# Expert rows stored and gathered, against rows added to the output by indirect accumulating transfers

## The chip, the cores and the metric

The kernel runs on one core of a Trainium2 chip. The metric is the device time of one execution in microseconds; the kernel before was timed three times: 2560.4 us median, 2554.97 to 2566.02.

## The reference, cut to what matters

The program is two transformer blocks over 256 tokens of 2048 features in fp32. The last stage of the second block is a mixture of experts. Each token goes to one group of 8 experts out of 4 groups and, inside it, to the two experts with the largest logits; each expert is a gated layer 2048 -> 256 -> 2048.

```
weights = softmax(top_val) * p_group                  # (token, 2)
act     = silu(xb @ w_gate[e]) * (xb @ w_up[e])       # rows of expert e
ys      = act @ w_down[e]
m       = sum over the token's 2 rows of weights * ys
x       = x + gate2 * m                               # the output
```

Everything ahead of this stage is untouched by the change.

## The kernel before, in words

The stage is cut into 48 tiles of 32 rows. Each of the 32 experts has one tile (even numbers of experts at tile % 3 == 0, odd ones at tile % 3 == 2), and the 16 tiles with tile % 3 == 1 are spare ones for rows beyond 32 of an expert. Which expert a spare serves is known only on the chip; where it serves none, its weights are not loaded, yet the tile is computed all the same on what lies in the buffer, and its rows are used by nobody.

A tile needs three weight units of 2 MB: two for gate and up, one for down. They live in `moe_raw`, two slots of three units: slot 0 serves tiles 3i and 3i+1, slot 1 serves tiles 3i+2. SyncE's queue loads the experts' tiles (L2797), each unit as soon as its slot is free (L2840: `e.free`), and GpSimd issues the spares' loads under a condition (L2801), after tile 3i has used the same units (L2849).

TensorE's order per tile: `up` on two units (L2876, 32-row weights, four row strips of PSUM, one for each quarter of the contraction), `fold` that adds the four strips (L2887), `down` (L2899), and between them `gather`, which picks the rows of a later tile out of the normalized tokens by a one-hot product (L2866, L2867). `down` puts output columns 512q to 512q+511 of its 32 rows into strip q of one bank, 128 partitions by 512. ScalarE makes `part` (L2958) and `silu` (L2952). VectorE makes `hidden` (L3021), half of the `spread` (L3014), the one-hot `places` (L2991, L2995), and `take` (L3027), which multiplies the tile's output by the gate and puts it into one of eight `moe_stage` buffers.

The stage buffer is stored to a DRAM tensor `expert_rows` of 1536 rows by four transfers per tile that ScalarE issues (L2964), two tiles later in its order. After the last tile a second block follows: GpSimd waits for all stores, and gathers for each half of the tokens and each of the two choices 128 rows of 8 KB by an indirect transfer (L3059); VectorE multiplies them by the token's weight and adds them to `x` (L3069); SyncE writes `x` to the output (L3080) and waits for it.

Of the kernel before, what the change touches and what calls it, by code (L numbers as in the profile page):

```python
# [43 lines left out]
MOE_SLOTS = MOE_TILES * ROWS  # L44
MOE_SPARE = MOE_TILES - EXPERTS
D_EXPERT = 256
MOD_COLS = 6 * D
# [22 lines left out]
for _name, _n in (("slot", MOE_SLOTS), ("fold", ROWS), ("steps", 7), ("start", EXPERTS),  # L70
                  ("jump", EXPERTS), ("earlier", EXPERTS + 1), ("tile", 1)):
    MOE[_name] = (_at, _n)
    _at += _n
# [76 lines left out]
def bank(k, b):  # L150
    return k.psum[:, b, :]
# [2399 lines left out]
class Sorting:  # L2551
# [6 lines left out]
    def __init__(self, sb):  # L2558
        self.const = sb("sorting", [P, N_MOE])
        self.slot = sb("slot_of", [P, TT, 2])  # L2560
        self.weight = sb("weight_of", [P, TT, 2])
        self.row = sb("row_of", [P, TT, 2], dtype=mybir.dt.int32)
        self.spare_of, self.filled = (sb(n, [P, 1], dtype=mybir.dt.int32) for n in ("spare_of", "spare_filled"))
# [6 lines left out]
def route(nc, k, x, x_t, xn_hi, router, scope_sb, first_loads):  # L2570
# [88 lines left out]
    with nc.Block(no_gpsimd_drain=True) as block:  # L2659
        @block.vector  # L2660
        def _(dve):
# [62 lines left out]
            s.settle()  # L2724
            s.step(dve.tensor_copy(sorting.row[:], sorting.slot[:]))

# [32 lines left out]
class Experts:  # L2759
# [9 lines left out]
    def __init__(self, k, weights, sb, sem):  # L2769
        self.k, self.weights = k, weights  # L2770
        self.raw = sb("moe_raw", [P, 2, self.UNITS, UNIT])
        self.unit_in = [[sem(f"moe_unit_in{slot}_{u}") for u in range(self.UNITS)] for slot in range(2)]
        self.spare_in = [sem(f"moe_spare_in{u}") for u in range(self.UNITS)]
        self.used_up, self.used_down, self.parts = sem("moe_used_up"), sem("moe_used_down"), sem("moe_parts")
        self.folded, self.silu_done, self.hid_done = sem("moe_folded"), sem("moe_silu_done"), sem("moe_hid_done")
        self.gathered, self.x_act, self.x_dve = sem("moe_gathered"), sem("moe_x_act"), sem("moe_x_dve")
        self.staged, self.y_done, self.x_low = sem("moe_staged"), sem("moe_y_done"), sem("moe_x_low")
        self.row_in = [sem(f"moe_row_in{n}") for n in range(2 * TT)]
        self.stored = [sem(f"moe_stored{n}") for n in range(self.STAGED)]

    def buffers(self, sb):
        self.place = sb("moe_place", [P, 2, TT, P], dtype=F32R)
        self.x_t = sb("moe_x_t", [P, 2, KC, P])
        self.part, self.silu = sb("moe_part", [P, 2, COLS]), sb("moe_silu", [P, 2, 2, ROWS])
        self.hid, self.stage = sb("moe_hid", [P, 2, 2, ROWS]), sb("moe_stage", [P, self.STAGED, COLS])

    @staticmethod
# [27 lines left out]

def experts(nc, k, io, e, x, xn_hi, xn_lo, sorting, scale, shift, gate_rows):
    s = k.dve_steps
    quads = MOE_TILES // 4
# [13 lines left out]
    def strip(n):  # L2832
        return slice(ROWS * n, ROWS * n + ROWS)
    with nc.Block(no_gpsimd_drain=True) as block:
        @block.sync
        def _(sp):
            for n in range(3, MOE_TILES):
                if n % 3 != 1:
                    for u in range(e.UNITS):
                        e.free(sp, n - 2 if n % 3 == 0 else n - 3, u)  # L2840
                        e.load(sp, n, u)

        @block.gpsimd
        def _(pool):
            for i in range(MOE_SPARE):
                at = pool.value_load(sorting.spare_of[i:i + 1, 0:1], min_val=0, max_val=e.UNITS * (EXPERTS - 1))
                filled = pool.value_load(sorting.filled[i:i + 1, 0:1], min_val=0, max_val=1)
                for u in range(e.UNITS):
                    e.free(pool, 3 * i, u)  # L2849
                    e.load_spare(pool, 3 * i + 1, u, at, filled)  # L2850

        @block.tensor
        def _(pe):
# [26 lines left out]
            def fold(tile):  # L2880
                pe.wait_ge(e.parts, tile + 1)
                if tile >= 2:
                    pe.wait_ge(e.hid_done, tile - 1)
# [7 lines left out]
            def down(tile):  # L2891
# [5 lines left out]
                for c in range(2):  # L2897
                    for q in range(4):
                        mm = pe.matmul(outs(tile)[strip(q), :], e.hid[:, tile % 2, c, :],  # L2899
                                       w[:, c * D + q * COLS:c * D + (q + 1) * COLS], start=c == 0, stop=c == 1)  # L2900
                mm.then_inc(e.used_down, 1)
            for g in range(3):
                gather(g)
            for tile in range(MOE_TILES):
# [14 lines left out]
                if shared_next:  # L2919
# [17 lines left out]
        def _(act):  # L2937
# [21 lines left out]

            def store(tile):  # L2960
                act.wait_ge(e.y_done, tile + 1)
                at = ROWS * Sorting.ORDER[tile]
                for q in range(4):
                    act.dma_start(io["rows"][at:at + ROWS, q * COLS:(q + 1) * COLS], e.stage[strip(q), tile % e.STAGED])\  # L2964
                       .then_inc(e.stored[tile % e.STAGED], 16)
            for g in (0, 2):
                spread(g)
            for tile in range(MOE_TILES):
# [5 lines left out]
                if tile % 2 == 0 and tile + 4 < MOE_TILES:  # L2974
                    spread(tile + 4)
                if tile >= 2:
                    store(tile - 2)
            silu(MOE_TILES - 1)
            store(MOE_TILES - 2)
            store(MOE_TILES - 1)  # L2980

        @block.vector
        def _(dve):
# [48 lines left out]
            places(1)  # L3032
            spread(3)
            for tile in range(MOE_TILES):
                if tile and tile % 3 != 1:
                    hidden(tile - 1)
                if tile % 3 == 0:
                    if tile:
                        take(tile - 1)
                    hidden(tile)  # L3040
                if tile % 2 and tile + 4 < MOE_TILES:
                    spread(tile + 4)
# [7 lines left out]
            take(MOE_TILES - 1)  # L3050
    rows = [[e.raw[:, 0, c, t * D:(t + 1) * D] for c in range(2)] for t in range(TT)]
    with nc.Block(no_gpsimd_drain=True) as block:
        @block.gpsimd
        def _(pool):
            for n in range(e.STAGED):
                pool.wait_ge(e.stored[n], 64 * len(range(n, MOE_TILES, e.STAGED)))
            for t in range(TT):
                for c in range(2):
# [4 lines left out]
        @block.vector  # L3063
        def _(dve):
            s.eng = dve
            for t in range(TT):
                for c in range(2):
                    dve.wait_ge(e.row_in[2 * t + c], 16)
                    ins = dve.scalar_tensor_tensor(x[:, t, :], rows[t][c], sorting.weight[:, t, c:c + 1], x[:, t, :],  # L3069
                                                   ALU.mult, ALU.add)  # L3070
                    if c == 0:
                        s.step(ins)
                        s.settle()
                ins.then_inc(k.out_ready, 1)

        @block.sync
        def _(sp):
            for t in range(TT):
                sp.wait_ge(k.out_ready, t + 1)
                sp.dma_start(io["out"][t * P:(t + 1) * P, :], x[:, t, :]).then_inc(k.out_written, 16)  # L3080
            sp.wait_ge(k.out_written, 16 * TT)


def program(nc, io):
    k = Kit(io["stream"])
    with ExitStack() as ctx:
# [7 lines left out]
        def sem(name):  # L3094
# [10 lines left out]
            sem("act_sem"), sem("pe_sem"), sem("consts_in")  # L3105
        k.out_ready, k.out_written, k.small_in = \
            sem("out_ready"), sem("out_written"), sem("small_in")
        k.row_high, k.row_low, k.row_used = sem("row_high"), sem("row_low"), sem("row_used")
# [189 lines left out]
        xn_hi, xn_lo = (sb(n, [P, TT, D], dtype=F32R) for n in ("xn_hi", "xn_lo"))  # L3298
        sorting = router.sorting
# [4 lines left out]
        experts(nc, k, io, moe, x, xn_hi, xn_lo, sorting, lambda c: scale2[:, c:c + 1],  # L3304
                lambda c: mod_cols[:, 32 + c:33 + c], gate_rows)
# [3 lines left out]
def lay_out(a):  # L3309
# [45 lines left out]
    for level in range(6):  # L3355
# [24 lines left out]
        "jump": np.broadcast_to(ROWS * (EXPERTS - 1 - experts), (P, EXPERTS)),  # L3380
        "earlier": m < np.arange(EXPERTS + 1), "tile": m,
    }
# [33 lines left out]
```

## Time and profile before

| What | Value |
|---|---|
| Median of three timed runs | 2560.4 us |
| Profiled execution, own time | 2563.39 us |
| Its span, first to last instruction | 2561.7 us |
| Mean granted TensorE clock | 0.918 of full speed |
| TensorE matmuls / VectorE / ScalarE / GpSimd busy | 2274.2 / 1331.5 / 789.4 / 21.5 us |
| Expert stage with its routing | from 1967 us to the end |

The span is what the profile's rows cover; some 1.7 us of the execution's own time lie outside it. Busy times are of the whole kernel and say little of one stage, so the rows below are mostly of stretches: the expert stage's steady part, one of its periods of three tiles, its start and its end. DMA share is the mean busy share of the 16 DMA engines.

### The profile page before, as it was taken

How to read it: one execution, taken by the hardware profiler on the slowest of the kernel's cores; microseconds unless marked ns; L12 is line 12 of the kernel's file. 1: busy time of each engine (PE TensorE's matmuls, PEld its weight loads, DVE VectorE, ACT ScalarE, POOL GpSimd, SP SyncE). 2: the span in 40 equal slices, each digit the busy share in tenths (PEclk: the TensorE clock that was granted, in tenths of full speed). 3: DMA queues.
4: the chain of work that ended last, by engine and by line, in shares of the span. 5: the costliest groups of instructions: out<-in, count | busy, mean ns of one | idle time of the engine just before them, and what ended most of it. 6: DMA issues, size and time to landing. Idle time of an engine off the chain costs nothing. (4 is left out here: it accounts for less than half of the span.)

```text
span 2561.7 us, 39746 instructions
## 1 busy us (share of the span) xinstructions
PE 2274.2 (89%) x17030; PEld 1832.3 (72%) x17030; DVE 1331.5 (52%) x1580; ACT 789.4 (31%) x917; POOL 21.5 (1%) x62
## 2 busy tenths in 40 slices
PE   7998799878889988999999999997978768888885
PEld 7998799677867657899999998976854424444441
DVE  4776655564453126878787978855543301111112
ACT  4444333311143024434334334345431101111110
POOL 0000000000000000000000000000000000000000
PEclk8999899887889998999999999998989768899987
DMA  4453034100053317888897888824522899999998
GB/s 201 184 197 132 2 131 197 58 2 1 2 207 154 132 66 273 325 320 322 303 356 300 338 327 325 343 107 196 197 84 106 330 418 420 427 423 428 426 427 337
DMA packets 68150, 610.05 MB, mean 238 GB/s; under 512 B 9614, under 2 KB 9870, under 8 KB 16782
## 3 DMA queue, kind: packets, MB, share of 16 engines
q1 hardware_dynamic: 56906, 572.11, 55.9%
q0 software_dynamic: 1872, 23.07, 2.2%
q10 hardware_dynamic: 9216, 12.60, 1.4%
q8 instruction: 121, 1.98, 0.3%
q14 instruction: 35, 0.29, 0.0%
HBM read 674.85 MB, written 14.68 MB: 269 GB/s over the span
## 5 line engine op out<-in xcount | busy, mean ns | idle before, releaser
L2051 ACT ACTIVATE ffn_w_hi<-ffn_raw 128x2048 fp32r<-128x2048 f32 x128 | 245.0, 1916 | 372.1 <-PE psum L2096 368.8
L2058 DVE TENSOR_TENSOR ffn_w_lo<-ffn_raw,ffn_w_hi 128x2048 fp32r<-128x2048 f32 x128 | 292.3, 2287 | 90.9 <-ACT ffn_w_hi L2051 90.9
L2094 PE MATMUL psum<-u_hi,ffn_w_hi 128*128 128x256 f32 x1024 | 294.0, 287 | 15.0 <-DVE ffn_w_lo L2058 13.9
L2876 PE MATMUL psum<-moe_raw,moe_x_t 128*32 128x512 f32 x1536 | 219.3, 703 | 83.9 <-DMA moe_raw<-in_moe 76.4
L2096 PE MATMUL psum<-u_hi,ffn_w_lo 128*128 128x256 f32 x1024 | 293.3, 286 | 0.0
L2095 PE MATMUL psum<-u_lo,ffn_w_hi 128*128 128x256 f32 x1024 | 293.3, 286 | 0.0
L613 DVE SCALAR_TENSOR_TENSOR shared<-mod_raw,c_silu,shared 128x2048 f32<-128x2048 f32 x96 | 225.0, 2344 | 0.0
L2094 PEld LDWEIGHTS psum<-u_hi,ffn_w_hi 128*128 128x128 f32 x1024 | 200.4, 196 | 15.8 <-DVE ffn_w_lo L2058 14.1
L2095 PEld LDWEIGHTS psum<-u_lo,ffn_w_hi 128*128 128x128 f32 x1024 | 200.3, 196 | 0.4
L2096 PEld LDWEIGHTS psum<-u_hi,ffn_w_lo 128*128 128x128 f32 x1024 | 200.2, 195 | 0.0
L2094 PE MATMUL psum<-ffn_w_hi,ffn_hid_hi 128*128 128x512 f32 x512 | 199.5, 390 | 0.0
L2095 PE MATMUL psum<-ffn_w_lo,ffn_hid_hi 128*128 128x512 f32 x512 | 199.4, 389 | 0.0
L2096 PE MATMUL psum<-ffn_w_hi,ffn_hid_lo 128*128 128x512 f32 x512 | 199.2, 389 | 0.0
L2876 PEld LDWEIGHTS psum<-moe_raw,moe_x_t 128*32 128x32 f32 x1536 | 49.1, 120 | 194.5 <-issue 154.1
L320 PE MATMUL psum<-dn_u_hi,dn_w_hi 128*128 128x256 f32 x512 | 146.5, 286 | 0.0
L322 PE MATMUL psum<-dn_u_hi,dn_w_lo 128*128 128x256 f32 x512 | 145.8, 285 | 0.0
L321 PE MATMUL psum<-dn_u_lo,dn_w_hi 128*128 128x256 f32 x512 | 145.8, 285 | 0.0
L3021 DVE TENSOR_TENSOR moe_hid<-moe_silu,psum 128x64 f32<-128x64 f32 x48 | 10.6, 221 | 213.0 <-ACT moe_silu L2952 213.0
L320 PE MATMUL psum<-rw_u_hi,rw_w_hi 128*128 128x256 f32 x384 | 110.1, 287 | 9.7 <-DVE rw_w_lo L309 9.7
L2866 PEld LDWEIGHTS psum<-moe_place,xn_hi 128*128 128x128 f32 x384 | 79.0, 206 | 46.7 <-issue 44.1
L2094 PEld LDWEIGHTS psum<-ffn_w_hi,ffn_hid_hi 128*128 128x128 f32 x512 | 96.2, 188 | 20.1
L2096 PEld LDWEIGHTS psum<-ffn_w_hi,ffn_hid_lo 128*128 128x128 f32 x512 | 96.1, 188 | 20.1
(579 smaller groups left out, 4344.5 us busy)
## 6 DMA issues: line engine op xcount, KB each, us to landing
moe_raw<-in_moe SPq DMA_DIRECT2D x96, 2048.0 KB, 17.2
ffn_raw<-in_ffn SPq DMA_DIRECT2D x128, 1024.0 KB, 5.5
ring<-in_stream SPq DMA_DIRECT2D x59, 2048.0 KB, 12.1
mod_raw<-in_mod SPq DMA_DIRECT2D x96, 1024.0 KB, 7.4
moe_raw<-in_moe POOLq DMA_DIRECT2D x48, 2048.0 KB
expert_rows<-moe_stage ACTq DMA_DIRECT2D x192, 64.0 KB, 8.5
x<-in_x SPq DMA_DIRECT2D x2, 1024.0 KB, 5.9
u<-in_mem SPq DMA_DIRECT2D x2, 1024.0 KB, 15.3
```

What stands on the lines that cost most here:

```text
L320: pe.matmul(out, hi, self.u_hi[:, chunk, :], start=chunk == 0, stop=False)
L321: pe.matmul(out, hi, self.u_lo[:, chunk, :], start=False, stop=False)
L322: mm = pe.matmul(out, lo, self.u_hi[:, chunk, :], start=False, stop=chunk == KC - 1)
L613: dve.scalar_tensor_tensor(at, self.raw[:, i % self.RAWS], self.c_silu[:, c:c + 1], at, ALU.mult, ALU.add)\
L2051: act.activation(self.w_hi[:, number % self.HIGHS], self.raw[:, number % self.RAWS], ACT.Copy)\
L2058: dve.tensor_tensor(self.w_lo[:, number % self.LOWS], self.raw[:, number % self.RAWS], self.w_hi[:, number % self.HIGHS].bitcast(F32), ALU ...
L2094: pe.matmul(out, lhs[0], rhs[0], start=start, stop=False)
L2095: pe.matmul(out, lhs[0], rhs[1], start=False, stop=False)
L2096: return pe.matmul(out, lhs[1], rhs[0], start=False, stop=stop)
L2866: pe.matmul(gathers(piece)[:, c, :], xn_hi[:, t, own], rows, start=t == 0, stop=False)
L2876: mm = pe.matmul(summed(tile)[strip(q), :], e.x_t[:, tile // 4 % 2, UNIT_KC * u + c, strip(tile % 4)], w[:, c * COLS:(c + 1) * COLS], star ...
L3021: dve.tensor_tensor(e.hid[:, tile % 2], e.silu[:, tile % 2], folds(tile)[:, 1], ALU.mult).then_inc(e.hid_done, 1)
```

## The change

Instead of 48 stored row blocks and a gather at the end, the unweighted residual `x` is written to the output at the start of the stage, and each tile adds its own rows to the output in memory.

- `Sorting` keeps each token's rank within its expert (`rank`) and no longer the integer row (`row`); the constants get a column `quarter`, m // 32 + 2048.
- VectorE runs a new function `hots` once, between `spread(3)` and tile 0: two `token` columns, a few steps on 128x4 values, and for each half of the tokens and each choice three comparisons against constants: a one-hot of the row in its tile (128x128) and two one-hots of the tile (128x48), scaled by the weight and by the token's number.
- TensorE runs `row_tables` once, after the last gather of tile 0's turn and before `down(0)`: four matmuls of 128x128 by 96 columns into a free part of bank 3. VectorE reads them after `hidden(0)`: a weight and an output row for each partition and tile. A row that holds no token gets number 2048 + q or more, which is past the last of the 1024 row quarters of the output.
- `take` becomes one SCALAR_TENSOR_TENSOR that multiplies by the row's weight and by the gate.
- GpSimd issues for every tile one indirect transfer of 128 pieces of 2 KB from the stage buffer to the output, with an add (`compute_op`), which leaves pieces out whose number is past the bound. Each waits until the one before it has landed. They stand in GpSimd's order behind the spare loads of their period: tiles 3i-1, 3i and 3i+1 behind the loads of tile 3i+1, and tile 47 last.
- ScalarE's stores, the DRAM tensor `expert_rows`, and the whole last block are gone; SyncE waits for the last accumulating transfer.

```diff
+    out_rows = io["out"].rearrange("t (q n) -> (t q) n", n=COLS)
+    def scatter(pool, tile):
+        pool.wait_ge(e.y_done, tile + 1)
+        if tile:
+            pool.wait_ge(e.scattered, 16 * tile)
+        pool.indirect_dma_start(out_rows, bass.IndirectOffsetOnAxis(ap=e.row_at[:, tile:tile + 1], axis=0),
+                                e.stage[:, tile % e.STAGED], None, bounds_check=4 * T - 1, oob_is_err=False,
+                                compute_op=ALU.add).then_inc(e.scattered, 16)
         def _(sp):
+            for t in range(TT):
+                sp.dma_start(io["out"][t * P:(t + 1) * P, :], x[:, t, :]).then_inc(k.out_written, 16)
...
+            sp.wait_ge(e.scattered, 16 * MOE_TILES)
         def _(pool):
...
                     e.load_spare(pool, 3 * i + 1, u, at, filled)
+                if i == 0:
+                    pool.wait_ge(k.out_written, 16 * TT)
+                    pool.wait_ge(e.rows_known, 1)
+                for tile in range(max(3 * i - 1, 0), 3 * i + 2):
+                    scatter(pool, tile)
+            scatter(pool, MOE_TILES - 1)
             def fold(tile):
                 pe.wait_ge(e.parts, tile + 1)
+                if tile == 1:
+                    pe.wait_ge(e.rows_known, 1)
+            def row_tables():
+                pe.wait_ge(e.hot_done, 1)
+                for n in range(2 * TT):
+                    mm = pe.matmul(bank(k, 3)[:, 256:256 + 2 * MOE_TILES], hot_row[:, n // 2, n % 2, :],
+                                   hot_tile[:, n // 2, n % 2].rearrange("p v n -> p (v n)"), start=n == 0, stop=n == 2 * TT - 1)
+                mm.then_inc(e.hot_mm, 1)
...
                         gather(tile + 4, range(2, 4))
+                    if tile == 0:
+                        row_tables()
                     down(tile)
-            def store(tile):
-                act.wait_ge(e.y_done, tile + 1)
-                at = ROWS * Sorting.ORDER[tile]
-                for q in range(4):
-                    act.dma_start(io["rows"][at:at + ROWS, q * COLS:(q + 1) * COLS], e.stage[strip(q), tile % e.STAGED])\
-                       .then_inc(e.stored[tile % e.STAGED], 16)
             def take(tile):
                 dve.wait_ge(e.used_down, tile + 1)
                 if tile >= e.STAGED:
-                    dve.wait_ge(e.stored[tile % e.STAGED], 64 * (tile // e.STAGED))
-                dve.tensor_tensor(e.stage[:, tile % e.STAGED], outs(tile), gate_rows[:], ALU.mult).then_inc(e.y_done, 1)
+                    dve.wait_ge(e.scattered, 16 * (tile - e.STAGED + 1))
+                dve.scalar_tensor_tensor(e.stage[:, tile % e.STAGED], outs(tile), e.row_weight[:, tile:tile + 1], gate_rows[:],
+                                         ALU.mult, ALU.mult).then_inc(e.y_done, 1)
+            def hots():
...
+                for t in range(TT):
+                    for c in range(2):
+                        dve.tensor_scalar(hot_row[:, t, c, :].rearrange("p (q r) -> p q r", r=ROWS),
+                                          starts[:, 0:1, :].broadcast_to([P, 4, ROWS]), row[:, t, c:c + 1], None, ALU.is_equal)
+                        dve.tensor_scalar(hot_tile[:, t, c, 0, :], starts[:, :, 0], first_row[:, t, c:c + 1],
+                                          sorting.weight[:, t, c:c + 1], ALU.is_equal, ALU.mult)
+                        ins = dve.tensor_scalar(hot_tile[:, t, c, 1, :], starts[:, :, 0], first_row[:, t, c:c + 1],
+                                                token[:, t:t + 1], ALU.is_equal, ALU.mult)
+                ins.then_inc(e.hot_done, 1)
-    rows = [[e.raw[:, 0, c, t * D:(t + 1) * D] for c in range(2)] for t in range(TT)]
...
-                    pool.indirect_dma_start(rows[t][c], None, io["rows"],
-                                            bass.IndirectOffsetOnAxis(ap=sorting.row[:, t, c:c + 1], axis=0))\
-                        .then_inc(e.row_in[2 * t + c], 16)
...
-                    ins = dve.scalar_tensor_tensor(x[:, t, :], rows[t][c], sorting.weight[:, t, c:c + 1], x[:, t, :],
-                                                   ALU.mult, ALU.add)
...
-                sp.dma_start(io["out"][t * P:(t + 1) * P, :], x[:, t, :]).then_inc(k.out_written, 16)
```

## Rows read from the trace of the kernel before

**Rows 1.** Windows: stretch, its us, busy of each engine, PEclk, DMA share, GB/s
```profile
2000.00:2010.00 10.00, 8.49 (x53) 6.04 (x56) 3.74 (x12) 1.50 (x4) 0.71 (x1) 0.73 0.16 36
2010.00:2042.00 32.00, 27.04 (x224) 12.73 (x220) 4.41 (x13) 7.20 (x16) 1.61 (x3) 0.95 0.93 368
2145.00:2530.00 385.00, 332.67 (x2607) 157.19 (x2602) 63.32 (x169) 55.94 (x142) 1.58 (x36) 0.91 1.01 426
2387.00:2418.00 31.00, 28.11 (x216) 13.72 (x216) 5.25 (x13) 3.74 (x9) 0.13 (x3) 0.90 1.01 428
```
**Rows 2.** Chain of waits, two successive periods: start us, us, what
```profile
2369.69 17.68 DMA moe_raw<-in_moe
...
2400.93 17.98 DMA moe_raw<-in_moe
```
**Rows 3.** The page's DMA queues: packets, MB, share of 16 engines' span
```profile
q0 software_dynamic: 1872, 23.07, 2.2%
q10 hardware_dynamic: 9216, 12.60, 1.4%
```
**Rows 4.** The page's DMA issues: transfer, issuer, count, KB each, us to landing
```profile
moe_raw<-in_moe SPq DMA_DIRECT2D x96, 2048.0 KB, 17.2
...
expert_rows<-moe_stage ACTq DMA_DIRECT2D x192, 64.0 KB, 8.5
```
**Rows 5.** The stores' line L2964 alone, from 2145 us: min/median/max to landing
```profile
DMA to landing us min/median/max: 1.6/8.6/13.9
```
**Rows 6.** Timeline of one period, GpSimd's skipped spare loads and VectorE's takes
```profile
2384.52 0.04 POOL L2801 DMA_DIRECT2D moe_raw<-in_moe  x1 [17.87 <-PE psum L2876]
2391.20 0.04 POOL L2801 DMA_DIRECT2D moe_raw<-in_moe  x1 [6.64 <-PE psum L2876]
2392.83 0.69 DVE L3027 TENSOR_TENSOR moe_stage<-psum,gate_rows 128x512 f32<-128x512 f32 x1 [7.19 <-PE psum L2899]
2397.26 3.62 PE L2876 MATMUL psum<-moe_raw,moe_x_t 128*32 128x512 f32 x32
2397.85 0.04 POOL L2801 DMA_DIRECT2D moe_raw<-in_moe  x1 [6.60 <-PE psum L2899]
...
2411.38 0.69 DVE L3027 TENSOR_TENSOR moe_stage<-psum,gate_rows 128x512 f32<-128x512 f32 x1 [0.52 <-PE psum L2899]
```
**Rows 7.** Timeline of the end
```profile
2519.06 0.69 DVE L3027 TENSOR_TENSOR moe_stage<-psum,gate_rows 128x512 f32<-128x512 f32 x1 [7.14 <-PE psum L2899]
...
2522.91 0.04 POOL L2801 DMA_DIRECT2D moe_raw<-in_moe  x1 [5.48 <-PE psum L2899]
...
2536.91 0.69 DVE L3027 TENSOR_TENSOR moe_stage<-psum,gate_rows 128x512 f32<-128x512 f32 x1 [2.47 <-PE psum L2899]
2541.52 1.00 POOL L3059 DMA_INDIRECT moe_raw<-expert_rows,row_of  x1 [18.57 <-DMA expert_rows<-moe_stage]
...
2547.22 2.35 DVE L3069 SCALAR_TENSOR_TENSOR x<-moe_raw,weight_of,x 128x2048 f32<-128x2048 f32 x1 [9.61 <-DMA moe_raw<-expert_rows,row_of]
...
2552.44 5.30 SPq L3080 DMA_DIRECT2D out<-x  x2
```
**Rows 8.** Timeline of the start: what stands around `hots` and `row_tables`
```profile
1988.91 0.16 DVE L2721 SCALAR_TENSOR_TENSOR slot_of<-of_row 128x4 f32<-128x4 f32 x1
...
2001.49 0.47 DVE L2991 TENSOR_SCALAR moe_place<-sorting,slot_of 128x128 fp32r<-128x128 f32 x2
...
2008.33 1.36 DVE L3014 TENSOR_SCALAR moe_x_t<-psum,scale,mod_cols 128x128 f32<-128x128 f32 x4 [5.72 <-PE psum L2867]
...
2013.95 0.22 DVE L3021 TENSOR_TENSOR moe_hid<-moe_silu,psum 128x64 f32<-128x64 f32 x1 [4.25 <-ACT moe_silu L2952]
```
**Rows 9.** Line L2740: small matmuls, min/median/max ns
```profile
L2740 PE MATMUL psum<-consts,any_of x4: 420/421/421, 1983.8 to 1984.4; 128*32 128x128 f32 x4
```

More of the change, by code:

```diff
@@ L45 @@
 MOE_SPARE = MOE_TILES - EXPERTS
+NO_ROW = 8 * T
 D_EXPERT = 256
@@ L70 @@
 for _name, _n in (("slot", MOE_SLOTS), ("fold", ROWS), ("steps", 7), ("start", EXPERTS),
-                  ("jump", EXPERTS), ("earlier", EXPERTS + 1), ("tile", 1)):
+                  ("jump", EXPERTS), ("earlier", EXPERTS + 1), ("tile", 1), ("quarter", 1)):
     MOE[_name] = (_at, _n)
@@ L2561, in __init__ @@
         self.weight = sb("weight_of", [P, TT, 2])
-        self.row = sb("row_of", [P, TT, 2], dtype=mybir.dt.int32)
+        self.rank = sb("rank_of", [P, TT, 2])
         self.spare_of, self.filled = (sb(n, [P, 1], dtype=mybir.dt.int32) for n in ("spare_of", "spare_filled"))
@@ L2724, in _ @@
             s.settle()
-            s.step(dve.tensor_copy(sorting.row[:], sorting.slot[:]))
+            s.step(dve.tensor_copy(sorting.rank[:], of_row[:, :, :, 0]))
             dve.wait_ge(k.act_sem, k.act_n + 3)
@@ L2777, in __init__ @@
         self.staged, self.y_done, self.x_low = sem("moe_staged"), sem("moe_y_done"), sem("moe_x_low")
-        self.row_in = [sem(f"moe_row_in{n}") for n in range(2 * TT)]
-        self.stored = [sem(f"moe_stored{n}") for n in range(self.STAGED)]
+        self.hot_done, self.hot_mm, self.rows_known = sem("moe_hot_done"), sem("moe_hot_mm"), sem("moe_rows_known")
+        self.scattered = sem("moe_scattered")
     def buffers(self, sb):
@@ L2785, in buffers @@
         self.hid, self.stage = sb("moe_hid", [P, 2, 2, ROWS]), sb("moe_stage", [P, self.STAGED, COLS])
+        self.row_weight, self.row_at = sb("moe_row_weight", [P, MOE_TILES]), sb("moe_row_at", [P, MOE_TILES], dtype=mybir.dt.int32)
     @staticmethod
@@ L2813, in first_loads, with experts @@
                 self.load(sp, n, u)
-def experts(nc, k, io, e, x, xn_hi, xn_lo, sorting, scale, shift, gate_rows):
-    s = k.dve_steps
+def experts(nc, k, io, e, x, xn_hi, xn_lo, router, scale, shift, gate_rows):
+    s, sorting = k.dve_steps, router.sorting
+    spare = router.w_norm[:].rearrange("p c n -> p (c n)")
+    hot_row = spare[:, 0:512].rearrange("p (t c n) -> p t c n", t=TT, c=2)
+    hot_tile = spare[:, 512:512 + 8 * MOE_TILES].rearrange("p (t c v n) -> p t c v n", t=TT, c=2, v=2)
+    over = spare[:, 900:928].rearrange("p (t c n) -> p t c n", t=TT, c=2)
+    earlier, row, first_row = (spare[:, 928 + 4 * n:932 + 4 * n].rearrange("p (t c) -> p t c", t=TT) for n in range(3))
+    token = spare[:, 940:942]
+    out_rows = io["out"].rearrange("t (q n) -> (t q) n", n=COLS)
     quads = MOE_TILES // 4
@@ L2975, in _ @@
                     spread(tile + 4)
-                if tile >= 2:
-                    store(tile - 2)
             silu(MOE_TILES - 1)
-            store(MOE_TILES - 2)
-            store(MOE_TILES - 1)
         @block.vector
@@ new lines, in hots @@
+            def hots():
+                steps, ranks = sorting.of("steps"), sorting.rank[:]
+                starts = sorting.of("slot").rearrange("p (n r) -> p n r", r=ROWS)
+                for t in range(TT):
+                    s.step(dve.tensor_scalar(token[:, t:t + 1], sorting.of("tile"), 4.0, float(4 * P * t - NO_ROW), ALU.mult, ALU.add))
+                s.step(dve.tensor_tensor(over, ranks.unsqueeze(3).broadcast_to([P, TT, 2, 7]),
+                                         steps.unsqueeze(1).unsqueeze(1).broadcast_to([P, TT, 2, 7]), ALU.is_gt))
+                s.settle()
+                s.step(dve.tensor_reduce(earlier, over, AX.X, ALU.add))
+                s.settle()
+                s.step(dve.scalar_tensor_tensor(row, earlier, -float(ROWS), ranks, ALU.mult, ALU.add))
+                s.settle()
+                s.step(dve.tensor_scalar(row, row, -1.0, None, ALU.add))
+                s.settle()
+                s.step(dve.tensor_tensor(first_row, sorting.slot[:], row, ALU.subtract))
+                s.settle()
+                for t in range(TT):
+                    for c in range(2):
[6 more added lines that the diff above has]
+                ins.then_inc(e.hot_done, 1)
@@ L3028, in _, with row_tables @@
+            def row_tables():
+                dve.wait_ge(e.hot_mm, 1)
+                s.step(dve.tensor_copy(e.row_weight[:], bank(k, 3)[:, 256:256 + MOE_TILES]))
+                dve.tensor_scalar(e.row_at[:], bank(k, 3)[:, 256 + MOE_TILES:256 + 2 * MOE_TILES], sorting.of("quarter"), None,
+                                  ALU.add).then_inc(e.rows_known, 1)
+                s.settle()
             places(0)
@@ L3033, in _ @@
             spread(3)
+            hots()
             for tile in range(MOE_TILES):
@@ L3040, in _ @@
                     hidden(tile)
+                    if tile == 0:
+                        row_tables()
                 if tile % 2 and tile + 4 < MOE_TILES:
@@ L3050, in _ @@
             take(MOE_TILES - 1)
-    rows = [[e.raw[:, 0, c, t * D:(t + 1) * D] for c in range(2)] for t in range(TT)]
[L3052 to L3058, printed above, removed]
-                    pool.indirect_dma_start(rows[t][c], None, io["rows"],
-                                            bass.IndirectOffsetOnAxis(ap=sorting.row[:, t, c:c + 1], axis=0))\
-                        .then_inc(e.row_in[2 * t + c], 16)
[L3063 to L3068, printed above, removed]
-                    ins = dve.scalar_tensor_tensor(x[:, t, :], rows[t][c], sorting.weight[:, t, c:c + 1], x[:, t, :],
-                                                   ALU.mult, ALU.add)
[L3071 to L3079, printed above, removed]
-                sp.dma_start(io["out"][t * P:(t + 1) * P, :], x[:, t, :]).then_inc(k.out_written, 16)
-            sp.wait_ge(k.out_written, 16 * TT)
 def program(nc, io):
@@ L3105, in program @@
             sem("act_sem"), sem("pe_sem"), sem("consts_in")
-        k.out_ready, k.out_written, k.small_in = \
-            sem("out_ready"), sem("out_written"), sem("small_in")
+        k.out_written, k.small_in = sem("out_written"), sem("small_in")
         k.row_high, k.row_low, k.row_used = sem("row_high"), sem("row_low"), sem("row_used")
@@ L3298, in program @@
         xn_hi, xn_lo = (sb(n, [P, TT, D], dtype=F32R) for n in ("xn_hi", "xn_lo"))
-        sorting = router.sorting
         with ExitStack() as routing:
@@ L3303, in program @@
         moe.buffers(sb)
-        experts(nc, k, io, moe, x, xn_hi, xn_lo, sorting, lambda c: scale2[:, c:c + 1],
+        experts(nc, k, io, moe, x, xn_hi, xn_lo, router, lambda c: scale2[:, c:c + 1],
                 lambda c: mod_cols[:, 32 + c:33 + c], gate_rows)
@@ L3380, in lay_out @@
         "jump": np.broadcast_to(ROWS * (EXPERTS - 1 - experts), (P, EXPERTS)),
-        "earlier": m < np.arange(EXPERTS + 1), "tile": m,
+        "earlier": m < np.arange(EXPERTS + 1), "tile": m, "quarter": m // ROWS + NO_ROW,
     }
@@ L3411 @@
     io["out"] = nc.dram_tensor("out", (T, D), F32, kind="ExternalOutput").ap()
-    io["rows"] = nc.dram_tensor("expert_rows", (MOE_SLOTS, D), F32).ap()
     program(nc, io)
```

## The prediction

> **What bounds the kernel now.** I read the stretches first, since the page's busy shares mix stages. In the steady part of the expert stage the DMA share is 1.01 at 426 GB/s, while TensorE is busy 333 of 385 us and VectorE 63 [rows 1]: the 16 DMA engines are full, and time goes by what they carry. The chain of waits says the same: it stands in a load of `moe_raw` for 17.68 us of a period, and the same place comes 31.24 us later [rows 2]. A period is three tiles, two with weights: 6 units of 2.097 MB are 12.58 MB, and 3 tiles of stores 0.79 MB; 13.37 MB in 31.24 us are 428 GB/s, the rate of the row. So the stores displace weights byte for byte, and they are worth reading as time. TensorE's 28.1 busy of 31 us [rows 1] is the next bound, 2.9 us below.
>
> How many spares are filled can be read too: GpSimd's queue moved 23.07 MB [rows 3], of which the last gathers are 4 x 1.05 = 4.19 MB, and 18.87 MB are left, three tiles of 6.29 MB. So 35 of 48 tiles hold rows, 13 periods have an empty spare, 3 a filled one.
>
> The end of the kernel is a serial tail. The last `take` ends at 2537.60; then come the last stores, four gathers, four sums of 2.35 us and the output's write, to the end of the span, 2561.7: 24.1 us in which TensorE does nothing [rows 7].
>
> **Part 1, the tail (on the path, all of it).** What remains after the last `take` is one indirect issue, its landing, and SyncE's wait. An indirect issue of 128 rows takes 1.00 us; the first gather, of 1.05 MB, was in after 5.7 us from its issue's start [rows 7]; a store on an idle machine landed in 1.6 us [rows 5]. So one scatter with no loads beside it costs between 1.0 + 1.6 = 2.6 and 5.7 us; a quarter of the bytes speaks for the low end, reading the target first for the high one; I take 4.0, and 3.0 for one without rows. The scatters are serial, however, and tile 44's waits behind the last spare load, 2522.9 [rows 7]. It still lies beside loads, so I give it issue 1.0 plus the stores' 8.6 [rows 5]: lands 2532.5. Tile 45: 4.5, 2537.0. Tile 46 (empty spare): 3.0, 2540.0. Tile 47: 4.0, 2544.0, plus 0.2 for the wait: 2544.2. Saved: 2561.7 - 2544.2 = 17.5 us. Without the lag it would be 20; if each of the four took 8.6 + 1.0 it would be 2561.3, so nothing.
>
> **Part 2, the stream.** Removed are the stores: 1.4% of 2561.7 = 35.9 us of all 16 engines [rows 3], for 48 x 128 / 16 = 384 pieces of 2 KB per engine, 93 ns each with their completions. This is real time wherever the share is 1.01. Added are the pieces that hold rows, 512 rows x 4 = 2048, or 128 per engine if they fall evenly. They may not: full pieces are the first of each strip of 32 partitions, and an engine that serves 8 fixed partitions can have all 8 full in each of 35 tiles, 280. A load is in only when its slowest engine is. The price of a piece with an add isn't in the trace: at least a stored piece's 93 ns, at most, with the target read as well as the source, twice that, 187. Both ends: 128 x 93 = 11.9 us, stream -24.0; 280 x 187 = 52.4, stream +16.5. Nothing nearer separates them, so I take the middle of both factors, 204 x 140 ns = 28.6 us: stream 28.6 - 35.9 = -7.3. TensorE has room for it: even -24 is 1.5 us a period, less than the 2.9 above.
>
> The row shows stores priced like loads, by bytes [rows 1, 3]. The Trainium skill (Collectives: The Full Stack, "The bandwidth ceiling") says that an add costs twice, because two sources are read through one ring, and (DMA: Bandwidth & Descriptors, "The descriptor swizzle") that a 128-partition transfer gives each engine eight fixed partitions, four neighbours in each of two strips. By both rules the high end holds, and the sum of all parts would be about zero; by a one-pass price on even engines it would be some -40. No row of this kernel shows an add in a transfer. This is rival 1.
>
> The written `x` (2.1 MB, 4.9 us at 426 GB/s) is issued behind the first loads and falls in a stretch with share 0.16 at 36 GB/s [rows 1], where nothing is in line; cost 0. Were that cover gone, 4.9.
>
> ScalarE loses 4 issues a tile. With DMA full, buffers that come free earlier bring nothing: 0. `take` stays one instruction of 128x512; a third operand of one column can leave it at 0.69 or, if it ran twice as long, take 0.7 more beside some 3 idle us per `take` [rows 6]: 0.
>
> **Part 3, the order on GpSimd.** Behind each scatter's wait stand the next spare loads, and behind them, through slot 0, SyncE's. In the shown period the last spare load is issued at 2397.85, the next period's first is due at 2384.52 + 31.24 = 2415.8, and its tile is multiplied at 2397.26 + 31.24 = 2428.5 [rows 6]. With a latency L for a scatter with rows, the three issue at 2397.9, 2397.9 + L, and the later of 2397.9 + 2L and 2412.1 (the `take`). For L: the stores, the nearest transfer, four issues of the same 128 pieces, took 8.6 in the median, 13.9 at most, beside the loads [rows 5]; with the issue 9.6 to 14.9; I take 9.6 for the median. Then the third issues at 2417.1 and GpSimd is free at 2418.1, 2.3 us after the next load was due, but 10 us before its weights are wanted; for an empty spare nothing is lost. Three filled periods have a real load that goes in 2.3 us later; a unit takes 17.2 us to land, 3.5 times its own 4.9 [rows 4], so the engines have work queued meanwhile: 0, at worst 3 x 2.3 = 7. From 2397.9 + 2L + 1 > 2428.5, L above 14.8, TensorE waits (rival 2).
>
> **Part 4, the start.** `hots` is 8 small steps, some 0.2 us each with their wait (the routing's run at that pace, 0.16 a step [rows 8]), 1.6 us, and 12 comparisons, four of 128x128 at 0.24 and eight smaller at 0.15 to 0.24: 2.2 to 2.9; together 3.8 to 4.5. VectorE is idle for 4.25 us just there, before `hidden(0)` [rows 8], so 0 to 0.3 is left. `row_tables` is 4 matmuls, 8 instructions. Two of 128 columns, in four instructions, took about 1.06 us (0.2 apart, 0.42 long) [rows 9]; for 8 of 96 columns, 8 x 0.2 = 1.6 at that pace, less at a higher clock; 1.2 taken. It stands before `down(0)`, in a stretch whose DMA share is 0.93, the machine being about to run dry. All on the path: +1.5, between 0 and 2.2. The two reads of bank 3 on VectorE, about 0.5 us, are past `hidden(0)` and before `fold(1)`, which waits for weights anyway.
>
> **Sum.** -17.5 - 7.3 + 1.5 = -23.3 us. The profiled execution took 2563.39, its span 2561.7, so after: 2540.1 and 2538.4. It lies 3.0 above the median of three, so against the median the forecast is 2560.4 - 23.3 = 2537.1. Lower bound -20 - 24 + 0 = -44 (2516).
>
> **The rivals.**
> 1. *The slowest engines hold the weight stream.* Full pieces crowd on few engines and cost double: +16.5, sum +0.5, 2561. For: full rows are always the first of a strip; share already 1.01. Against: queued loads let an engine be behind for a while, and pieces may be dealt out otherwise.
> 2. *The serial scatters take the place of DMA as the bound (slower).* Beside loads an add reads the target before it writes, so L may exceed the stores' maximum. Place: the spare load behind the third scatter. From L = 14.8 on. A period is then 2L plus 3 for the empty one; at L = 16, 35 against 31.24: 13 x 3.8 = +49 us, sum +33, 2594. Against: the stores' median 8.6; for: each scatter waits for the last piece of the slowest engine, 48 times.
> 3. *Past-the-end pieces are not left out.* 384 per engine at 93 to 187 ns: 35.9 to 71.8, stream 0 to +36, sum -16 to +20; 2544 to 2580.
> 4. *The tail keeps its length.* Four scatters at 8 us lag to about 2555: tail -7, sum -13, 2547.
>
> **How the numbers follow.** A change of 0.5%, 12.8 us, is about what can be told from none. Forecast 0.55 (own range 2516 to 2547), rival 1 0.17, rival 2 0.13, rival 3 0.05, rival 4 0.10. Faster by over 0.5%: the forecast and a third of rival 4, 0.58. Slower: rival 2, half of rival 3 and some of rival 1 with a price above 187 ns, 0.19. The rest, 0.23, within. Range: 2518 leaves out only the all-good corner, 2576 takes in rival 1 with an overrun and most of rival 3; outside are rival 2 beyond small excess and the corner, under 0.2.
>
> **What would show it.** Tail: from the last `take` to the end 5 to 8 us. Stream: the period in the chain of waits near 30.8 (30.3 to 31.2 by the forecast; 32.3 by rival 1), the share at 1.0. GpSimd: scatters' issue to landing near 8.6 in the steady part; above 13.8 with TensorE waiting at unfilled spares is rival 2. The queue of GpSimd should carry some 23 MB (18.9 of loads, 4.2 of rows); about 31 would be rival 3. Start: `down(0)` later by 1 to 2 us. The forecast is wrong if the period is over 31.24 or the tail over 12 us.

## The result, and the profile after

The changed kernel takes 2583.3 us in the median of five runs (2576.6 to 2588.0) against 2562.1 for the kernel before, a ratio of 1.0078 (95% interval 1.006 to 1.0096): slower by 21 us, where the prediction gave 23 us less than before. The profiled execution took 2576.6 us, the fastest of the five, with a span of 2574.9.

The starts of the 48 `take`s cut the stage into pieces. They are worked out from VectorE's timelines in the two profiled executions, in us:

| Piece | before | after | difference |
|---|---|---|---|
| first `places` to first `take` | 26.0 | 26.9 | +1.0 |
| tiles 0 to 12 (three filled spares) | 158.9 | 162.1 | +3.2 |
| tiles 12 to 45, 11 periods | 347.2 | 366.2 | +19.0 |
| tiles 45 to 47 | 14.3 | 21.4 | +7.1 |
| last `take` to the end | 24.8 | 11.8 | -13.0 |

The stage began 4.0 us earlier in the profiled run, so the span grew by 13.2. The tail is indeed shorter; the stream of weights in front of it lost more. First the steady windows of after (columns as in [rows 1]), whole and one period:

```profile
2145.00:2530.00 385.00, 314.80 (x2451) 149.53 (x2444) 62.60 (x163) 53.59 (x137) 53.30 (x67) 0.90 0.97 387
...
2313.00:2346.00 33.00, 26.82 (x216) 13.12 (x216) 6.65 (x18) 3.97 (x10) 4.70 (x6) 0.95 0.96 376
```

Against [rows 1] the share fell from 1.01 to 0.97 and the rate from 426 to 387 GB/s: the stores' bytes are gone (0.79 MB in 31.24 us are 25 GB/s of it), and the DMA engines are no longer full, so something else sets the pace. GpSimd's timeline of one period names it:

```profile
2313.02 1.54 POOL L2849 DMA_INDIRECT out<-moe_stage,moe_row_at  x1 [10.77 <-DMA out<-moe_stage,moe_row_at]
...
2321.12 1.54 POOL L2849 DMA_INDIRECT out<-moe_stage,moe_row_at  x1 [5.92 <-DMA out<-moe_stage,moe_row_at]
2334.55 1.54 POOL L2849 DMA_INDIRECT out<-moe_stage,moe_row_at  x1 [11.89 <-DMA out<-moe_stage,moe_row_at]
2347.22 1.54 POOL L2849 DMA_INDIRECT out<-moe_stage,moe_row_at  x1 [11.13 <-DMA out<-moe_stage,moe_row_at]
2348.51 0.04 POOL L2803 DMA_DIRECT2D moe_raw<-in_moe  x1
...
2355.36 1.54 POOL L2849 DMA_INDIRECT out<-moe_stage,moe_row_at  x1 [5.95 <-DMA out<-moe_stage,moe_row_at]
```

Each scatter (as the accumulating transfers are called from here on) is issued some 0.8 us after the one before it has landed. In this period it is 13.4 and 12.7 us from issue to issue for the two with rows and 8.1 for the empty spare's, 34.2 us in all against a period of 31.2 before. Over tiles 12 to 45 the 33 links of this chain take 365 us, which is the stretch's own 366.2: in the median 12.3 us with rows and 10.0 (7.8 to 12.2, one of 6.0) for an empty spare. The spare load (L2803), skipped though it is, stands behind the third scatter, and TensorE starts on that tile 0.15 us later, having waited 6.75 us:

```profile
2348.66 5.81 PE L2903 MATMUL psum<-moe_raw,moe_x_t 128*32 128x512 f32 x32 [6.75 <-DMA moe_raw<-in_moe]
```

Over all 48 (line L2849 alone, durations in ns), with the page's chain and GpSimd's queue:

```profile
L2849 POOL DMA_INDIRECT out<-moe_stage,moe_row_at x48: 1531/1538/1749, 2015.1 to 2570.0; - x48
...
DMA to landing us min/median/max: 2.7/11.2/34.6
```
```profile
q0 software_dynamic: 8208, 23.11, 2.8%
...
DMA out<-moe_stage,moe_row_at 18%; PE psum L2903 1%; DMA moe_raw<-in_moe 1%; PE psum L2893 0%; PE psum L2894 0%; PE psum L2928 0%; POOLq L2867 0%; POOL out L2849 0%; PE psum L2916 0%; DVE moe_stage L3055 0%; DVE xn_lo L3031 0%; POOLq L2849 0%; POOLq L2868 0%; PE psum L2935 0%; POOLq L2848 0%
```

Before, the chain stood in `moe_raw` loads (11% of the span on its page); now it stands in the scatters. The queue carried 23.1 MB, so the bytes of pieces past the end are left out. The end of the kernel shows the idle-machine cost of a scatter, and the same hold-up a last time:

```profile
2548.23 6.73 PE L2903 MATMUL psum<-moe_raw,moe_x_t 128*32 128x512 f32 x48 [6.59 <-DMA moe_raw<-in_moe]
...
2563.11 0.75 DVE L3055 SCALAR_TENSOR_TENSOR moe_stage<-psum,moe_row_weight,gate_rows 128x512 f32<-128x512 f32 x1 [2.05 <-PE psum L2928]
2566.50 1.54 POOL L2849 DMA_INDIRECT out<-moe_stage,moe_row_at  x1 [3.35 <-DMA out<-moe_stage,moe_row_at]
2570.01 1.54 POOL L2849 DMA_INDIRECT out<-moe_stage,moe_row_at  x1 [1.98 <-DMA out<-moe_stage,moe_row_at]
```

With no loads beside them a scatter with rows takes 4.9 us (2570.01 to the span's end at 2574.9) and one without rows 3.5 (2570.01 less 2566.50). From issue to landing these are 4.4 and 2.7.

### The profile page after: what moved, and what is told of

It is laid out like the page before. It is cut to its first block and busy times, and to the rows that moved or that the text cites. A ratio compares the mean times of both kernels' runs of the same rounds, so it can differ in the third digit from the quotient of the medians.

```text
span 2574.9 us, 39709 instructions
## 1 busy us (share of the span) xinstructions
PE 2262.4 (88%) x17038; PEld 1823.7 (71%) x17038; DVE 1329.5 (52%) x1597; ACT 789.4 (31%) x917; POOL 91.8 (4%) x106
## 3 DMA queue, kind: packets, MB, share of 16 engines
q0 software_dynamic: 8208, 23.11, 2.8%
## 5 line engine op out<-in xcount | busy, mean ns | idle before, releaser
L2996 ACT ACTIVATE moe_part<-psum 128x512 f32<-128x512 f32 x48 | 28.7, 598 | 283.3 <-PE psum L2903 283.3
L3049 DVE TENSOR_TENSOR moe_hid<-moe_silu,psum 128x64 f32<-128x64 f32 x48 | 10.6, 221 | 199.4 <-ACT moe_silu L2990 199.4
## 6 DMA issues: line engine op xcount, KB each, us to landing
ring<-in_stream SPq DMA_DIRECT2D x59, 2048.0 KB, 12.2
```

The costliest lines, as they stand in the source:

```text
L2996: act.activation(e.part[:, tile % 2], summed(tile), ACT.Copy).then_inc(e.parts, 1)
```

## The experiments

Two theories stand against each other. Theory A: the serial chain on GpSimd, with the spare loads queued in it, holds the weights. Theory B: pieces with rows crowd on few DMA engines at twice the price, and the slowest engine holds the weights. All edits are to the kernel after, unless said; the code is shortened, `...` stands for what is left out, and the comments in it are mine. Ratios are to the kernel before, run on the same chip; microseconds between two rows of the table can come from two chips, on which the kernel before took 2562 to 2564. The pieces and landings are of one profiled execution each. e3, e7, e8, e11 and e12 leave the rows of the three filled spares out of the output, and e4 loses rows; the others write the whole output.

| Run | median us | ratio (95%) | 12 to 45 | last `take` to end | landing, median |
|---|---|---|---|---|---|
| after | 2583.3 | 1.0078 (1.006 to 1.0096) | 366.2 | 11.8 | 11.2 |
| e1 spares by sync | 2579.3 | 1.0062 (1.0044 to 1.0079) | 347.1 | 33.8 | 11.3 |
| e2 even rows | 2572.0 | 1.003 (1.0017 to 1.0043) | 359.6 | 8.8 | 10.8 |
| e3 no spare scatter | 2552.7 | 0.9954 (0.9937 to 0.9972) | 350.2 | 9.3 | 11.5 |
| e5 half packets | 2557.8 | 0.9981 (0.9972 to 0.9991) | 353.7 | 11.5 | 8.9 |
| e4 plain write | 2536.6 | 0.989 (0.9866 to 0.9914) | 339.3 | 6.6 | 8.2 |
| e7 release order, no spare scatter | 2598.1 | 1.0136 (1.0106 to 1.0165) | 393.1 | 6.6 | 11.6 |
| e8 the same, even rows | 2590.5 | 1.01 (1.0076 to 1.0123) | 388.2 | 5.2 | 11.1 |
| e6 even, half, release order | 2600.0 | 1.0141 (1.0116 to 1.0166) | 389.3 | 5.2 | 8.5 |
| e12 tile order, no spare scatter | 2546.2 | 0.9941 (0.9924 to 0.9959) | 349.5 | 6.5 | 11.6 |
| e11 the same, even rows | 2533.1 | 0.9884 (0.9868 to 0.9901) | 339.7 | 5.3 | 11.1 |
| e10 even, half | 2543.0 | 0.9927 (0.991 to 0.9943) | 346.2 | 8.2 | 8.5 |
| e9 even, half, tile order | 2539.9 | 0.991 (0.9893 to 0.9926) | 346.8 | 6.0 | 8.7 |
| e13 before, half packets | 2568.0 | 1.0019 (1.0005 to 1.0033) | 347.3 | 25.0 | 6.1 |
| e14 even, quarter | 2565.0 | 1.0005 (0.9992 to 1.0019) | 357.3 | 5.3 | 7.5 |

**e1, spare loads on SyncE.**
```diff
-                    e.load_spare(pool, 3 * i + 1, u, at, filled)   # GpSimd: only the 48 scatters are left
+                    e.load_spare(sp, 3 * i + 1, u, at, filled)     # SyncE: tile 3i+1, then 3i+3, 3i+5
```


> Edit: the 16 spare loads are issued by SyncE in the order in which their buffers come free; GpSimd does nothing but the 48 serial scatters. Theory A (order on GpSimd: the next spare loads stand behind a serial chain whose links take about 12 us with rows and 8 without, 2 x 12 + 8 = 32 to 33 us against a period of 31.2): the weight stream is free again, its period falls from 32.4 to 31.2 or less, the chain lags up to some 20 us, which eight stage buffers cover, and the 10 us lost before the last two tiles come back; span 2545 to 2555 against 2575. Theory B (pieces with rows crowd on few DMA engines at twice the price, and the slowest engine holds the weights): the period stays above 32 us, span 2562 to 2570.

The steady window of e1, then GpSimd at its end:

```profile
2145.00:2530.00 385.00, 333.60 (x2590) 156.55 (x2584) 67.07 (x172) 55.22 (x140) 49.39 (x32) 0.90 1.00 407
```
```profile
2543.06 1.54 POOL L2849 DMA_INDIRECT out<-moe_stage,moe_row_at  x1 [2.00 <-DVE moe_stage L3053]
2548.41 1.54 POOL L2849 DMA_INDIRECT out<-moe_stage,moe_row_at  x1 [3.81 <-DMA out<-moe_stage,moe_row_at]
...
2570.84 1.54 POOL L2849 DMA_INDIRECT out<-moe_stage,moe_row_at  x1 [1.97 <-DMA out<-moe_stage,moe_row_at]
```

The stream is back at 347.1 us and a share of 1.00: the queueing of the spare loads is what held it, as A says. The total missed its range by over 20 us. The chain now lags behind instead: after the last `take`, at 2542.0, seven more scatters follow, and the last two `take`s already waited 3.2 and 2.0 us for one of the eight stage buffers. Tiles 12 to 47 take 27.2 us less than in after, and the tail 22.0 more: most of the microseconds are owed at the end instead of in the middle. The chain's own length is the bound, and the order only decides where it is paid. Another 5.7 us were lost ahead of tile 12 (167.8 against 162.1, and 167.8 in e3 too); no run shows why.

**e3, no scatter for spare tiles** (the rows of the three filled spares are left out of the output).
```diff
+        if tile % 3 == 1:
+            return
```


> Edit: no scatter is issued for the 16 spare tiles (the rows of the three filled spares are left out of the output). Theory A: the chain is 2 x 12 = 24 us a period, below the stream's 31, GpSimd is at its spare loads in time, span 2543 to 2552. Theory B: 13 of the 16 carry no rows and the other three few, so the slow engines keep their load: span 2562 to 2572.

It takes 30.6 us less than after, at the upper edge of what A says (span 2552.1): two links of 12 us fit into a period, three don't, although 13 of the 16 scatters that are gone carry nothing.

**e2, even rows.**
```diff
-        "slot": ... (ROWS * order[:, None] + np.arange(ROWS)) ...
+        "slot": ... (ROWS * order[:, None] + np.arange(ROWS) // 4 + 8 * (np.arange(ROWS) % 4)) ...
```


> Edit: the constant table of slots is permuted inside each tile (rank r of an expert sits at position 4 (r mod 8) + r div 8 of the 32), so that the full rows of a tile spread over all neighbourhoods of partitions instead of the first ones. Theory B: the most loaded engine falls from some 262 pieces of 187 ns to about 130, so 20 to 25 us come off: span 2550 to 2555. Theory A: each engine still has eight pieces of every scatter, left out or not, each of which takes its turn between load packets, so the landing of a scatter stays near 11 us and the span within 5 us of 2575.

It takes 11 us less than after, which lies between the two theories. While the chain is the bound it can't size B; e11 and e12 do.

**e5, expert units in two transfers of 8 KB per partition.**
```diff
+        for h in range(2):
+            own = slice(h * HALF, (h + 1) * HALF)
+            sp.dma_start(self.raw[:, slot, u, own], self.weights[..., :, own])
```


> Edit: each expert weight unit is loaded by two transfers of 8 KB per partition instead of one of 16 KB (the spare units stay whole), so a DMA engine's turn on the load queue is about 0.31 us instead of 0.61. Theory A with turns (a scatter has eight pieces per engine and each waits one load packet): a scatter's landing falls by 8 x 0.3 = 2.4 us, from 11.2 to about 8.8 in the median, the chain to 27 us a period, below the stream, and the span to 2550 to 2558. Theory B: the same bytes on the same engines, span 2575 within 4; likewise if a scatter's time is latency of its own and not turns.

The landing is 8.9 us in the median and the kernel takes 25.5 us less, both as A with turns says. The control is e13, the same halves in the kernel before:

> Edit: the kernel before, with the expert units loaded in halves as in the runs above and nothing else. If the halves help only through the scatters' turns: the stores land sooner (8.6 to some 6.5 us) but nobody waits for them, so the time stays within 4 us of before, or is a little worse since small packets cost about 1% more engine time (309 x 2 against 611 ns): 2562 to 2570. If the loads themselves gain, it is 10 us or more faster than before.

It is 5 us slower than before (a ratio of 1.0019, clear of 1), so halved loads gain nothing of themselves; they shorten the scatters. Quarters are e14:

> Edit: GpSimd's order kept, even rows, expert units in quarters of 4 KB per partition; output whole. Turns: eight waits of about 0.16 us instead of 0.31, so the median landing falls from 8.5 to about 7.2 us; the chain is below the stream already, so the span stays near 2538, or rises by up to 10 for more packets and more issues on SyncE. If landing doesn't fall, a scatter's time is not made of turns.

With even rows the landing is 10.8, 8.5 and 7.5 us for load pieces of 16, 8 and 4 KB:

```profile
DMA to landing us min/median/max: 2.7/10.8/35.2
```
```profile
DMA to landing us min/median/max: 2.7/8.5/24.5
```
```profile
DMA to landing us min/median/max: 2.7/7.5/12.5
```

A load piece costs an engine about 0.61 us at 16 KB (2.1 MB at 428 GB/s are 4.9 us for 8 of them). Eight such turns are 4.9, 2.5 and 1.2 us, steps of 2.4 and 1.2, where 2.3 and 1.0 were measured. The level needs one term more. With no loads, a scatter of even rows lands after 3.2 us:

```profile
DMA to landing us min/median/max: 3.2/3.2/3.2
```

This is e2's tile 47. The traces' records of single DMA packets, from which I worked out medians over tiles 15 to 41, show that beside loads the first packet of a scatter starts 4.7 us after the issue at all three sizes, and 2.1 us after it with no loads: 2.6 us more. The sum 3.2 + 2.6 + 4.9, 2.5 or 1.2 is 10.7, 8.3 and 7.0, against 10.8, 8.5 and 7.5. So a scatter's time beside loads is its idle time, a later start, and about eight turns behind a load piece.

Pieces that are left out take turns too. The queue holds a packet for each of them: e1's queue of scatters alone has 6912 packets, 48 x (128 + 16), of which the records show 2048 of 2 KB and 4096 of 8 bytes. An empty scatter's packets pass in 0.26 us with no loads, and in 3.9 us beside loads in after and 5.4 in e1 (medians over the same tiles); it lands after 2.7 us with no loads and 10.6 in e1.

Quarters are too much of it: e14's landing of 7.5 is near its 7.2, but its span of 2561.5 lies 13 us above its range, and the stream takes 11 us more than in e10. Whether the 384 issues on SyncE or the smaller packets cost that was not separated.

**e4, scatters without the add** (rows overwrite each other and x).
```diff
-                                compute_op=ALU.add).then_inc(e.scattered, 16)
+                                ).then_inc(e.scattered, 16)
```


> Edit: the 48 scatters write without the add (so a token keeps the rows of one expert only and loses x; order, waits and pieces as after). What the add itself costs in the chain: by the trace of after 187 ns a piece against a stored piece's 87, so up to 8 x 0.1 = 0.8 us a scatter, plus the read of the target. If turns between load packets make up the time, landing stays at 10 to 10.6 us of 11.2 and the span at 2562 to 2570; if the read-modify-write makes it, landing falls to the stores' 8.6 or below and the span to 2555 or less.

```profile
L2849 POOL DMA_INDIRECT out<-moe_stage,moe_row_at x48: 974/974/1123, 2023.3 to 2531.7; - x48
...
DMA to landing us min/median/max: 2.1/8.2/30.2
```
```profile
q0 software_dynamic: 5136, 23.09, 2.3%
```

Without the add a scatter lands 3 us sooner, of which 0.56 us are GpSimd's own time, and the queue takes 2.8% of 2574.9 less 2.3% of 2534.8 = 13.8 us less of the engines' time. The kernel takes 46.7 us less than after and 28 less than before. But the run changes more than the add. The queue has 5136 packets for 8208, and with the spare loads' 1296 taken off (8208 less e1's 6912) that is 80 a scatter for 144: pieces go two to a packet, those with rows mostly as one of 4 KB (980 in the records). So up to four of the eight turns, 2.4 us, are gone too, and what the read of the target costs by itself is not shown.

**e7, e8, e6: SyncE in the order in which buffers come free** (e7 and e8 without the spare tiles' rows).


> Edit: spare loads issued by SyncE, each unit in the order in which its buffer comes free, and no scatter for spare tiles (their rows are left out). Neither the chain (24 us a period) nor GpSimd's order can hold the weights, so this is the stream alone with uneven pieces. Theory A: period 31.5 as with the spare loads on SyncE before, last take near 2538 to 2541, tail 9, span 2545 to 2550. It is the base for the even version beside it.

> Edit: as the one beside it, with the slots permuted so that full rows fall evenly on all partitions. Theory B as a second cost (the most loaded engine's 262 double-price pieces against 130): period falls by (262 - 130) x 0.187 / 16 = 1.5 us, span 20 us under the uneven one, 2525 to 2530. If the engines' backlog evens out by itself: within 3 us of the uneven one.

> Edit: all three that keep the output whole: spare loads on SyncE in order of release, even rows, expert units loaded in halves. Chain 2 x 9.6 + 7 = 26 us a period, below the stream. Theory A: period 31.5 or a little less, no lag at the end, tail 8 to 9, span 2543 to 2550. With theory B as a second cost another 10 to 20 less, 2527 to 2538. If the chain is still too long: last take near 2540 and a tail of over 15.

All three took 45 to 60 us more than the upper end of their ranges. The steady window of e8, and who waited for what in it (us in total, times, longest):

```profile
2145.00:2530.00 385.00, 298.92 (x2368) 144.94 (x2360) 61.00 (x158) 52.64 (x134) 34.22 (x22) 0.84 0.90 362
```
```profile
PEld psum L2941 <- issue: 112.8, 96, 9.6
```

TensorE loses 113 us ahead of `down` (L2941), in stretches put down to issue, up to 9.6 us at a time; e11, with the order below and nothing else changed, has 38.1 there, none over 0.7. The `down` unit of tile 3i+3 was queued behind two `up` units of 3i+5, because their buffers came free earlier. e12 differs from e7 in that order alone (pairs of tile and unit):

```diff
+ (3i+1, 0), (3i+1, 1), (3i+2, 2), (3i+1, 2), (3i+3, 0), (3i+3, 1), (3i+3, 2), (3i+5, 0), (3i+5, 1)
```


> Edit: the same SyncE order, no scatter for spare tiles (their rows are left out), uneven rows, whole units. Stream alone with uneven pieces, neither chain nor GpSimd's order in the way: span 2545 to 2552.

It takes 52 us less than e7. So in this kernel loads are better queued in the order of use than in that of release.

**e11, the same with even rows.**


> Edit: as the one before it with even rows. Theory B as a cost of its own in a DMA-bound stream: 132 fewer double-price pieces of 187 ns on the most loaded engine, up to 20 us less than the uneven one; in the TensorE-bound pair it was 8. If the backlog evens out: within 3 us.

It takes 13.1 us less than e12, with no chain in the way. So B is real, as a second cost: 13 us, where up to 20 were expected. The crowding shows on the idle machine too: the last scatter's packets (20 pieces with rows) pass in 2.0 us in after and in 0.8 in e2.

**e10 and e9, whole outputs.**


> Edit: the whole change with GpSimd's order kept, even rows and expert units in halves; output whole. The halves took 18 us off and the even rows 7 in the spans, by different ways (fewer microseconds a turn; fewer double-price pieces on one engine). If the two are separate costs they add: span 2548 to 2552. If both only shortened the same chain, the second brings little once it is below the stream: 2555 to 2558.

> Edit: spare loads on SyncE again, but with the tiles' units in the order of before and each spare's first two units ahead of the third unit of the tile after it; even rows and halves as well; output whole. If the loss of the version in order of release came from that order (a unit for the next down queued behind two units of a later tile), it is gone: stream 12 to 45 near 347 us as with the first SyncE order, no lag of the chain (landing 8.9), tail 9, span 2540 to 2550. If SyncE is too slow at issuing itself, it stays above 2570.

```profile
2145.00:2530.00 385.00, 332.58 (x2609) 156.56 (x2608) 66.24 (x170) 56.10 (x143) 57.10 (x37) 0.91 1.01 407
```

Even rows bring 14.7 us on top of the halves (e10 against e5), and the two together 40.3 us against 11.3 and 25.5 alone, so the costs add. e10's span of 2537.9 lies 10 us below its range, e9's of 2538.3 just below its own. e9 computes everything: 2539.9 us, 0.9% under the kernel before; e10's 2543.0 can't be told from it (their intervals overlap). Its share, shown above, is 1.01 again and its tail 6.0 us.

## Why the prediction was wrong

- *Bound before* (DMA full, tail serial): right. e1, e9 and e13 return to 347 us for tiles 12 to 45, the stream's own time.
- *Part 1, tail*: direction right, -13.0 against -17.5. Idle scatters were 4.9 and 3.5 us against 4.0 and 3.0, and tile 45's, given as landed 0.6 us before the last `take` ended, had 2.6 us still to go.
- *Part 2, stream, -7.3*: too low by some 10 us. In e1 GpSimd's queue carries only scatters:
```profile
q0 software_dynamic: 6912, 4.23, 1.0%
```
  1.0% of 2575.8 is 25.8 us as a mean over the engines. The 28.6 of the prediction was meant for the fullest engine, so that the two are near is luck. 25.8 us are 201 ns for each piece with rows (25.8 x 16 / 2048), left-out pieces and completions included, twice the stored piece's 93, where I had taken 140. The crowding cost 13.1 us on top (e12 to e11), where the middle value of 204 pieces gave 76 x 140 ns = 10.6. Together that is 38.9 - 35.9 = +3.0, and tiles 12 to 45 agree: 347.1 in e1 and 349.5 in e12 against 347.2 before, so the stream gained nothing. Rival 1 was half right. The doubled price agrees with the rule of the Trainium skill (Collectives: The Full Stack, "The bandwidth ceiling") that the prediction had weighed, which that page states for a collective whose add reads two sources.
- *Part 3, the step that failed.* The order on GpSimd was given a cost of 0, at worst 7 us, because an empty scatter beside loads was put at 3.0 us and one with rows at 9.6. Measured from issue to issue they take 10.0 and 12.3 in the median, and tiles 12 to 47 lost 26 us. The prediction let TensorE wait from L = 14.8 on, a figure for one period that starts with nothing owed. As a chain, 2L + 3 exceeds 31.2 from L = 14.1 on, and with 10.0 for the empty one already from 10.6 on. This is rival 2, given 0.13: place and mechanism right, its point of decision wrong. The stores' 8.6 as the nearest row lacked what comes with the add (8.2 without it in e4, 11.2 with it), and the idle 3.0 was carried into a stretch where every piece, left out or not, queues behind loads.
- *Part 4, start*: +1.0 for +1.5; the `hots` took 3.9 us of the 4.25.
- *Rival 3* (pieces not left out): wrong by bytes, and yet they cost turns. *Rival 4*: no, the tail was 11.8 us, though e1 shows such a one, 33.8.

What stays open: why the first packet of a scatter comes 2.6 us later beside loads; what the read of the target costs by itself; the 5.7 us ahead of tile 12 in e1 and e3. The turns are inferred from three load sizes and the packets' times, since the records don't say which engine a packet ran on.

## What to carry to other kernels

Before a wait for completion goes between transfers, multiply its latency beside the real traffic by their count per period, empty ones included, and compare with the period; if it is close, shorten the turns (smaller load pieces) and keep nothing else behind the waiting instruction. Moving the other work off that queue only moved the debt to the end (e1), until the chain itself was shorter than the stream (e9; e10 shows that the move is then hardly needed). Here a piece with an add cost the engines twice a stored one, and dealing sparse rows evenly over the partitions, one line of a constant table, gave 8 to 15 us.

## What the runs showed of the hardware

- An indirect accumulating transfer of 128 pieces of 2 KB, some of them left out: 1.54 us on GpSimd and 11.2 us to landing beside full loads (after, median); without the add 0.97 and 8.2, with two pieces to a packet (e4).
- One with all pieces left out still has 128 packets of 8 bytes in its queue: 2.7 us to landing with no loads, 10.6 beside them (e1).
- A 2 KB piece takes 176 ns of an engine with the add (after, e1) and 84 ns as a store (before), medians of the packet records.
- The landing falls with the size of the pieces of an unrelated load queue: 10.8, 8.5, 7.5 us at 16, 8, 4 KB (e2, e10, e14).
- Loads in quarters cost the stream 11 us over tiles 12 to 45 (357.3 in e14 against 346.2 in e10), halves nothing (347.3 in e13 against 347.2 in the kernel before, though e13 as a whole is 5 us slower).
